# Doubling steps of a triangular inverse: products of odd heads moved to the crossed 64x64 tiles of the array

## The reference, cut to what matters

```
def step(S, inp):
    r_t, w_t, k_t, v_t, a_t, b_t = inp
    sa = jnp.einsum('bhvk,bhk->bhv', S, a_t)
    S = S * w_t[:, :, None, :] + sa[..., None] * b_t[:, :, None, :] + v_t[..., None] * k_t[:, :, None, :]
    return S, jnp.einsum('bhvk,bhk->bhv', S, r_t)
```

## Time and profile before

| | us |
|---|---|
| median of 3 runs | 517.11 |
| lowest, highest | 516.94, 517.74 |
| the profiled execution | 516.5 |
| its span | 514.7 |
| PE busy | 502.2 |
| PEld busy (beside PE) | 458.3 |
| DVE busy | 304.1 |
| ACT busy | 249.6 |
| POOL busy | 47.3 |

### The profile page before, as it was taken

The page is one execution under the profiler, slowest core; times in us unless marked ns, Lnnn a source line. Parts: engine busy times, 40 slices in busy tenths (PEclk is TensorE's granted clock), DMA queues, the critical chain, the costliest instruction groups (busy, mean ns, idle before and its releaser), DMA issues.

```text
span 514.7 us, 9588 instructions
## 1 busy us (share of the span) xinstructions
PE 502.2 (98%) x4064; PEld 458.3 (89%) x4064; DVE 304.1 (59%) x423; ACT 249.6 (48%) x379; POOL 47.3 (9%) x48
## 2 busy tenths in 40 slices
PE   3999999999999999999999999999999999999997
PEld 3989988988889878899999998899999999999995
DVE  4667897444453796436426986676555555555542
ACT  5677442555663235655424334564444454444440
POOL 1002003220570030000001220000000000000000
PEclk9999999999999999999999999999999999999999
DMA  9876452433422223344315646558666665666612
GB/s 256 264 213 190 135 168 83 124 100 106 125 82 83 74 70 105 113 115 124 120 46 165 194 138 204 161 166 223 196 193 187 185 196 171 193 188 193 199 46 82
DMA packets 101660, 76.87 MB, mean 149 GB/s; under 512 B 2545, under 2 KB 93297, under 8 KB 101618
## 3 DMA queue, kind: packets, MB, share of 16 engines
q1 hardware_dynamic: 101618, 76.26, 50.2%
HBM read 75.20 MB, written 1.05 MB: 148 GB/s over the span
## 4 chain that ended last, share of the span: by engine, by line
PE 92%; DVE 4%; DMA 1%; ACT 1%; issue 1%; SPq 0%; ACTq 0%
PE bank L460 26%; PE bank L461 24%; PE bank L462 24%; PE bank L667 2%; PE bank L685 2%; DMA stage<-in_w_in 1%; PE bank L696 1%; PE bank L553 1%; PE bank L774 1%; DVE mat L1141 1%; PE bank L731 1%; PE bank L720 1%; PE bank L712 1%; PE bank L730 1%; PE bank L634 1%
## 5 line engine op out<-in xcount | busy, mean ns | idle before, releaser
L1031 DVE TENSOR_TENSOR w_lo<-stage,w_hi 128x1024 fp32r<-128x1024 f32 x138 | 172.3, 1253 | 127.2 <-ACT w_hi L812 127.1
L812 ACT CAST w_hi<-stage 128x1024 fp32r<-128x1024 f32 x138 | 143.9, 1049 | 111.6 <-PE bank L462 83.9
L460 PE MATMUL bank<-h_hi,w_hi 128*128 128x256 f32 x656 | 192.5, 293 | 1.1 <-DVE h_lo L1055 0.8
L461 PE MATMUL bank<-h_lo,w_hi 128*128 128x256 f32 x656 | 185.7, 283 | 0.0
L462 PE MATMUL bank<-h_hi,w_lo 128*128 128x256 f32 x656 | 185.6, 283 | 0.0
L460 PEld LDWEIGHTS bank<-h_hi,w_hi 128*128 128x128 f32 x656 | 125.5, 191 | 10.1 <-issue 7.1
L461 PEld LDWEIGHTS bank<-h_lo,w_hi 128*128 128x128 f32 x656 | 125.7, 192 | 0.6
L462 PEld LDWEIGHTS bank<-h_hi,w_lo 128*128 128x128 f32 x656 | 125.6, 192 | 0.0
L460 PE MATMUL bank<-w_hi,r_hi 128*128 128x512 f32 x128 | 50.1, 391 | 0.0
L461 PE MATMUL bank<-w_lo,r_hi 128*128 128x512 f32 x128 | 50.1, 391 | 0.0
L462 PE MATMUL bank<-w_hi,r_lo 128*128 128x512 f32 x128 | 49.9, 390 | 0.0
(11 more groups left out here) (208 smaller groups left out, 632.8 us busy)
## 6 DMA issues: line engine op xcount, KB each, us to landing
stage<-in_w_ff SPq DMA_DIRECT2D x64, 512.0 KB, 4.2
stage<-in_w_in SPq DMA_DIRECT2D x54, 512.0 KB, 3.9
stage<-in_w_branch SPq DMA_DIRECT2D x12, 512.0 KB, 3.5
stage<-in_w_out SPq DMA_DIRECT2D x8, 512.0 KB, 3.4
xs<-in_x SPq DMA_DIRECT2D x2, 512.0 KB, 4.4
out<-xs SPq DMA_DIRECT2D x4, 256.0 KB, 2.1
cst<-in_consts SPq DMA_DIRECT2D x1, 897.0 KB, 7.4
lora<-in_g_up SPq DMA_DIRECT2D x1, 256.0 KB
```

Source lines behind the costliest of these rows:

```text
L460: pe.matmul(o, lh, rh, start=first, stop=False)
L461: pe.matmul(o, lh, rl, start=False, stop=False)
L812: nc.scalar.copy(w_hi[:, v % RING], stage[:, v % STAGES]).then_inc(hi_done, 1)
L1031: dve.tensor_tensor(w_lo[:, v % RING], stage[:, v % STAGES], w_hi[:, v % RING].bitcast(F32), ALU.subtract)\
```

## The change

The matmuls stay 16 a group with the same shapes; where they run changes. Head h = 2j + e. In the Y product, block b of head 2j + e still reads row half b, but its output goes to partition half e: an even head's block 0 and an odd head's block 1 stay on the diagonal, the other two cross. Y of row half b goes to its own bank, so a group fills two banks, with 256 columns in each. The masked Y (`y_q`) and the transpose (`xt_c`) are now laid out with the head's parity e as the row half and the block b as a column index. In the X product the operands lie in half e and the output goes back to half b, in bank e. Each of the two drains becomes two operations of half the columns. The transpose of X by L696 has just the layout of `xt_c`, so for levels 0 to 3 ACT takes it in one copy instead of four; for level 4 it still spreads it over `xt_e`. The masked copy for level 0 becomes four copies of 64 rows, two of which change the half. Since `xt_e` is no longer filled at the start, a memset writes its zero blocks before the corner step. The core of the diff:

```diff
@@ pe_uses
-            out += [(("Y", c, l),)]
+            out += [(("Y", c, l, b),) for b in range(2 if l < LEVELS else 1)]
-            out += [(("X", c, l),)]
+            out += [(("X", c, l, e),) for e in range(2)]
@@ build_layer
+        xt_c, y_q = (flat[:, o:o + 512].rearrange("p (j b s) -> p j b s", j=PAIRS, b=2) for o in (4096, 5632))
@@ tensor, quarter 0
-                        copied(pe, ("X", c, l - 1))
-                    o = room(pe, ("Y", c, l))
-                    for h in range(HEADS):
-                        if l < LEVELS:
-                            for b in range(2):
-                                rows = slice(HD * b, HD * b + HD)
-                                ins = pe.matmul(o[rows, HD * h:HD * h + HD], gm[rows, h, 0, rows], x_c[rows, h],
-                                                start=True, stop=True)
+                        for e in range(2):
+                            copied(pe, ("X", c, l - 1, e))
+                    if l < LEVELS:
+                        both = [room(pe, ("Y", c, l, b)) for b in range(2)]
+                        for j in range(PAIRS):
+                            for b, e in ((0, 0), (1, 1), (0, 1), (1, 0)):
+                                rows, to = (slice(HD * i, HD * i + HD) for i in (b, e))
+                                ins = pe.matmul(both[b][to, HD * j:HD * j + HD], gm[rows, 2 * j + e, 0, rows],
+                                                x_c[rows, 2 * j + e], start=True, stop=True)
+                                if (j, e) == (PAIRS - 1, 1 - b):
+                                    ins.then_inc(full_of(("Y", c, l, b)), 1)
@@ tensor, quarter 2
+                        for b in range(2):
+                            copied(pe, ("Y", c, l, b))
+                        both = [room(pe, ("X", c, l, e)) for e in range(2)]
+                        for j in range(PAIRS):
+                            for e, b in ((0, 0), (1, 1), (0, 1), (1, 0)):
+                                rows, to = (slice(HD * i, HD * i + HD) for i in (e, b))
+                                ins = pe.matmul(both[e][to, HD * j:HD * j + HD], xt_c[rows, j, b], y_q[rows, j, b],
+                                                 start=True, stop=True)
@@ scalar
-                    for b in range(2):
+                    if l < LEVELS - 1:
+                        ins = nc.scalar.copy(xt_c.rearrange("p j b s -> p (j b s)"), o[:])
+                    for b in range(2) if l == LEVELS - 1 else ():
...
-                        o = take(act, ("X", c, l))
-                        nc.scalar.copy(x_c, rows(o[:])).then_inc(drained_of(("X", c, l)), 1)
+                        for e in range(2):
+                            o = take(act, ("X", c, l, e))
+                            nc.scalar.copy(x_c.rearrange("p (j e) s -> p e j s", e=2)[:, e],
+                                           o[:, 0:256].rearrange("p (j s) -> p j s", j=PAIRS))\
+                              .then_inc(drained_of(("X", c, l, e)), 1)
@@ vector
-                    dve.tensor_tensor(xt_e[:, hs], gm[:, hs, 0], wide(cst[:, C_M1T:C_M1T + P], 4), ALU.mult)\
-                       .then_inc(xte_ready, 1)
+                    for b in range(2):
+                        for e in range(2):
+                            rows, to = (slice(HD * i, HD * i + HD) for i in (b, e))
+                            ins = dve.tensor_tensor(xt_c[to, 2 * g:2 * g + 2, b], gm[rows, 4 * g + e:4 * g + 4:2, 0, rows],
+                                                    wide(cst[rows, C_M1T + HD * b:C_M1T + HD * b + HD], 2), ALU.mult)
+                    ins.then_inc(xte_ready, 1)
...
-                        dve.tensor_tensor(y_c, rows(o[:]), wide(cst[:, C_LEV + HD * l:C_LEV + HD * l + HD], HEADS), ALU.mult)\
-                           .then_inc(drained_of(("Y", c, l)), 1)
+                        for b in range(2):
+                            o = take(dve, ("Y", c, l, b))
+                            dve.tensor_tensor(y_q[:, :, b], o[:, 0:256].rearrange("p (j s) -> p j s", j=PAIRS),
+                                              wide(cst[:, C_LEV + HD * l:C_LEV + HD * l + HD], PAIRS), ALU.mult)\
+                               .then_inc(drained_of(("Y", c, l, b)), 1)
                     else:
+                        dve.memset(xt_e[HD:P, :, 0:HD], 0.0)
```

More of the change, by code:

```diff
@@ L660, in extra @@
                     else:
-                        copied(pe, ("X", c, l - 1))
-                    o = room(pe, ("Y", c, l))
-                    for h in range(HEADS):
-                        if l < LEVELS:
-                            for b in range(2):
-                                rows = slice(HD * b, HD * b + HD)
-                                ins = pe.matmul(o[rows, HD * h:HD * h + HD], gm[rows, h, 0, rows], x_c[rows, h],
-                                                start=True, stop=True)
-                        else:
+                        for e in range(2):
[9 more added lines that the diff above has]
+                                    ins.then_inc(full_of(("Y", c, l, b)), 1)
+                    else:
+                        o = room(pe, ("Y", c, l, 0))
+                        for h in range(HEADS):
                             ins = pe.matmul(o[HD:P, HD * h:HD * h + HD], corner[:, h], x_c[0:HD, h], start=True, stop=True)
-                    ins.then_inc(full_of(("Y", c, l)), 1)
+                        ins.then_inc(full_of(("Y", c, l, 0)), 1)
                 if level_places(t) and p == 2:
@@ L677, in extra @@
                         copied(pe, ("XT", c, l - 1))
-                    copied(pe, ("Y", c, l))
-                    name = ("X" if l < LEVELS else "XT", c, l)
-                    o = room(pe, name)
-                    for h in range(HEADS):
-                        if l < LEVELS:
-                            for b in range(2):
-                                rows = slice(HD * b, HD * b + HD)
-                                ins = pe.matmul(o[rows, HD * h:HD * h + HD], xt_e[rows, h, rows], y_c[rows, h],
-                                                start=True, stop=True)
-                        else:
+                    if l < LEVELS:
+                        for b in range(2):
[5 more added lines that the diff above has]
+                                ins = pe.matmul(both[e][to, HD * j:HD * j + HD], xt_c[rows, j, b], y_q[rows, j, b],
+                                                start=True, stop=True)
+                                if (j, b) == (PAIRS - 1, 1 - e):
+                                    ins.then_inc(full_of(("X", c, l, e)), 1)
+                    else:
+                        copied(pe, ("Y", c, l, 0))
+                        o = room(pe, ("XT", c, l))
+                        for h in range(HEADS):
                             ins = pe.matmul(o[0:HD, HD * h:HD * h + HD], y_c[HD:P, h], xt_e[HD:P, h, HD:P],
                                             start=True, stop=True)
-                    ins.then_inc(full_of(name), 1)
+                        ins.then_inc(full_of(("XT", c, l)), 1)
                 if level_places(t) and p == 0 and level_places(t)[1] > 0:
@@ L1153, in extra @@
                     c, g, _ = before
-                    hs = slice(4 * g, 4 * g + 4)
                     dve.wait_ge(nt_ready, 2 * c + g + 1)
-                    dve.tensor_tensor(xt_e[:, hs], gm[:, hs, 0], wide(cst[:, C_M1T:C_M1T + P], 4), ALU.mult)\
-                       .then_inc(xte_ready, 1)
+                    for b in range(2):
[4 more added lines that the diff above has]
+                    ins.then_inc(xte_ready, 1)
                 if level_places(t) and p == 0:
@@ L1160, in extra @@
                     rows = lambda v: v.rearrange("p (h s) -> p h s", h=HEADS)
-                    o = take(dve, ("Y", c, l))
                     if l < LEVELS:
-                        dve.tensor_tensor(y_c, rows(o[:]), wide(cst[:, C_LEV + HD * l:C_LEV + HD * l + HD], HEADS), ALU.mult)\
-                           .then_inc(drained_of(("Y", c, l)), 1)
-                    else:
-                        dve.tensor_copy(y_c[HD:P], rows(o[HD:P])).then_inc(drained_of(("Y", c, l)), 1)
+                        for b in range(2):
[3 more added lines that the diff above has]
+                               .then_inc(drained_of(("Y", c, l, b)), 1)
+                    else:
+                        o = take(dve, ("Y", c, l, 0))
+                        dve.memset(xt_e[HD:P, :, 0:HD], 0.0)
+                        dve.tensor_copy(y_c[HD:P], rows(o[HD:P])).then_inc(drained_of(("Y", c, l, 0)), 1)
                 if t in S_APPLY:
```

## The result

The changed kernel takes **511.72 us** in the median of 4 runs (510.58 to 512.65), the kernel before 517.03 in 4 runs beside it (516.56 to 517.74): a ratio of 0.9897, 95% interval 0.9873 to 0.9921. It is faster, by 5.3 us (1.0 per cent) and not by the 8.7 of the forecast.

What follows compares the result with a forecast made beforehand. PE was taken as the bound, busy 502.2 of 514.7 us. The groups' -9.2 and the masked copy's +0.45 gave -8.75 us, hence 508.4 us against a median of 517.11; range 506.6 to 515.0.

Steps and rivals of the forecast that it cites:

- twenty groups, in turn over four tiles: Y and X products on PE: each group falls from 1.08 to 0.62 us, giving back 9.2 us in all.
- masked copy in four, by itself: DVE copy starting XT: four operations take 1.14 us instead of 0.67, one of them on the path, +0.45 us.
- Y in two drains, X in two, XT in one, memset: Drains on DVE and ACT and the memset: Y's two take 0.85 us, but all is hidden, costing nothing.
- A: Matmul records of four tiles cannot start that close together; at 0.022 us spacing the kernel takes 512.8 us; chance 0.13.
- B: Crossed tiles wait for diagonal ones, so nothing is gained and DVE's 0.45 us is added: 517.6 us; chance 0.07.
- C: The array empties at each of seven changes between diagonal and crossed pairs in a group: 530 us; chance 0.05.
- The clock row shows PE at its full 2.4 GHz throughout: Reading of the earlier profile's clock row, made when judging what bounds the kernel; no cost was attached.
- Each has room: Weight supply in the level stretches: ACT, DVE and the DMA engines can each deliver 8 per cent more.
- 0.2 us left: First level of chunk 1: Y's cover before the X group shrinks from 1.3 to 0.7, then 0.2 us; still hidden.
- Rival D: PE, early, meets Y, X or the DVE stretch, 0.2 to 0.3 us in ten groups: 511 us; chance 0.08.
- the likeliest case: The forecast itself, with the groups' gain and the masked copy's cost: 508.4 us, range 506.6 to 509.8, chance 0.67.
- the values are as many: Masked copy on DVE: reason given for the lower bound of its growth, nothing, against an upper bound of 0.47 us.

Runs made afterwards that it cites:

- r2_before_split_poolwait: Kernel before with only the masked copy cut in four, and POOL's second identity addition waiting until the four are done: 517.81 us, ratio 1.001.
- r1_before_split: Kernel before with only the masked copy of four heads cut into four copies, its groups unchanged: 520.64 us, ratio 1.006.
- r1_poolwait: Changed kernel with POOL's second identity addition of a chunk waiting until the first half's four masked copies are done: 509.42 us, ratio 0.9841.
- r1_late: Changed kernel with both halves' masked copies moved behind the y_lo that PE waits for: 510.03 us, ratio 0.9855.
- r2_best: Changed kernel with the first half's masked copies behind y_lo and POOL's second identity addition waiting for DVE's weight split: 508.66 us, ratio 0.9836.
- r2_g0late: Changed kernel with only the first half's masked copies moved behind y_lo, without a wait on POOL: 508.49 us, ratio 0.9832.
- r3_best: The same program as r2_best, run again beside the changed kernel and the kernel before: 507.40 us, ratio 0.9809 to the kernel before.

## Why the prediction was right, and where it was wrong

| Step | Forecast, us | Shown, us |
|---|---|---|
| twenty groups, in turn over four tiles | -9.2 | -9.06 |
| masked copy in four, by itself | +0.45 | +0.5 (`r2_before_split_poolwait`; 0.05 to 1.0) |
| POOL's operation beside the copies | not named | +1.1 (wait 2.0 instead of 0.9) |
| the clock behind the wait | not named | +1.7 in nearly every run, by the mean clock twice that in some |
| Y in two drains, X in two, XT in one, memset | 0 | no wait of PE |
| sum | -8.75 | -5.8 (medians of before and after in three comparisons: -5.3, -5.8, -5.4) |

**The groups** were right to 0.01 us each (0.62 forecast, 0.625 measured). The reasons held as well: a group lasts as long as its busiest tile's records, and the two kinds of pair in the earlier trace rows together allow four. Rivals A, B and C are out: 0.015 us in the mean is below A's floor, a group isn't 1.08, and the seven changes between diagonal and crossed pairs cost nothing that can be seen. The Trainium skill's floor of about 25 ns from start to start ("TensorE: Matmul & The Clock Gate", "Wait — 56ns, not 53.3ns?") doesn't hold over four tiles: 32 records would need 0.78 us by it, and took 0.476. Nor does the rule of "The mechanism" on the same page, by which weight loads overlap only across row groups; the crossed tiles share their rows with diagonal ones and run beside them. The trace of before could have taken most of rival A's chance away: by the single starts in the group of the earlier trace rows, where two tiles take turns, each record of the second tile starts 0.007 us behind one of the first. Rival A looked only at means over a group.

**The sum's +0.45 for the masked copy is the step that failed.** The working took the four copies' durations from L1147, which reads PSUM, and they were right. What it didn't ask is who else would start in the row of four. The earlier trace rows showed one operation of 0.67; POOL's own row, with an operation that started inside it, was not looked at, nor was the `w_lo` behind, which took 1.73 there where its mean is 1.25: the collision stood in the trace of before. The single operation, under way first, held POOL off (1.59 instead of 1.27); four short ones have gaps, and POOL's came into the first of them (into the second in `r1_before_split`) and kept the next copy standing until it was done. `r1_poolwait` takes exactly that away: 2.23 to 1.18 us, wait 2.0 to 0.9. The Trainium skill has the rule ("SBUF — State Buffer", "SBUF: two separate sides"): a DVE operation with two SBUF inputs and a GpSimd operation that reads SBUF share a pair of ports, and whichever starts first keeps them for its whole instruction. The trace agrees: the copy and `w_lo`, both from SBUF, were stretched to 1.34 and 2.03 us, the L1157 out of PSUM by no more than 0.02. Read against the change, that rule would have put POOL's 1.27 us on the list of what the four copies can meet; 1.1 of it was lost.

**"The clock row shows PE at its full 2.4 GHz throughout" was read and then assumed to stay so.** In the changed kernel PE's idle time before `y_lo` grew to 2.0 us, and behind it stood 3.4 us at the lower level. Kernels with 1.7 or 2.0 us of wait there have a mean clock of 0.997 or less in every run but that first profile; `r1_late`, `r2_best` and `r2_g0late`, with 1.1 at most, in none of 17 runs, `r1_poolwait` and `r2_before_split_poolwait`, with 0.9 and 0.7, in 2 of 16 (0.997). What sets the fall in a single run stays open.

**"Each has room"** held: neither PE stretch got a wait from DVE, ACT or the DMAs. The Y drains took 0.75 for two in a row, not 0.85. At the place with "0.2 us left", L1183's two end at 195.79 and L691 starts at 197.06, 1.3 later, as much as before. PE had been held up by the same DVE stretch as Y: in `r2_best`, where PE waits 0.4 instead of 2.0, L1183's two end at 194.42 and L691 starts at 195.06, 0.64 later. So the cover does shrink to the 0.7 of the working, but not to 0.2: in the kernel before, DVE idled 0.45 us for ACT behind the second masked copy of chunk 1, and the longer copy goes into that gap.

```profile
195.04 0.75 DVE L1183 TENSOR_TENSOR mat<-bank,cst 128x256 f32<-128x256 f32 x2
...
197.06 0.34 PE L691 MATMUL bank<-mat 64*64 64x64 f32 x8
```

**Rival D** has nearly the measured time, 511, but not its cause. It had many small waits of Y and X in chunk 1's levels; there was one wait, in the DVE stretch, and the clock. It was also the only rival with the right idea, that DVE would take back part of the gain.

**The range** of 506.6 to 515.0 held, and that is in part luck. The range of the likeliest case, 506.6 to 509.8, would not have held: it had no room for a term that wasn't in the sum. The room above it was made for A and D, and what filled it was neither.

## What to carry to other kernels

When one operation on a shared path is cut in pieces, look at what the other engines could start in the gaps, POOL first where both read SBUF; and move short work off the places where the dense engine waits, since a wait of 2 us may cost nearly as much again in clock. Small matmuls are worth putting in all four tiles, but in turn: the same records tile by tile were slower than two tiles.

## What the hardware showed that I had not expected

- Four 64x64 tiles take 32 records in 0.476 us, 0.015 apart in the mean; the order of issue sets the overlap: 0.63 us a group in turn, 0.68 in blocks of four records, 1.47 in blocks of eight.
- After 1.7 to 2.0 us of PE waiting in otherwise dense work, the granted clock was at 1.2 GHz for 3.4 us (a stretch of four at 0.57); by the mean clocks that happened in 24 of 25 runs.
- PE's matmuls reach full spacing at about 12 us in some executions and at about 16 in others, of one and the same program too (`r2_best` and `r3_best`), while the column of the granted clock shows full in both. The runs of before lie in two heaps (516.5 and 517.7 for instance), 1.2 us apart, as the two starts would make them, and a comparison of a few runs carries that error.
- DVE's 64x128 copy from SBUF takes 0.29 us, like one out of PSUM (0.286 in the earlier trace rows), where the 128x512 one takes 0.67. The text on the change calls each of the four a quarter of the values. It is a quarter of the columns, on half the partitions, an eighth of the values (the zero blocks are left out), so "the values are as many" in the prediction is wrong too. I read the time as going by the columns and an entry for each operation, not by the partitions. No row of DVE changes the partitions alone; ACT's copies out of PSUM take 0.367 for 64x256 and 0.369 for 128x256.
